# Per-head query norms of an attention layer: two root-mean squares taken in one PSUM bank and spread by copies, rotation ahead of the plain part

## What is computed

```python
def rms_norm(x, gain):
    y = xf * lax.rsqrt(jnp.mean(xf * xf, axis=-1, keepdims=True) + RMS_EPS)
    return (y * gain).astype(x.dtype)

q = (rms_norm(c_q, q_norm_g) @ w_qb).reshape(B, S, H, 192)
q = rms_norm(q, q_head_g)                    # per head, over all 192 features
q = concatenate([q[..., :128], rope(q[..., 128:], pos)], axis=-1)
# k likewise (one rotated part for all heads); logits = q k^T / sqrt(192),
# block-causal mask, softmax over k, times v
```

## Time and profile before

| | us |
|---|---|
| median of 3 runs | 4075.6 |
| lowest and highest run | 4072.52, 4077.5 |
| the profiled execution | 4080.59 |
| span of its slowest core (core 2) | 4079.6 |
| spans of the other cores | 4057.6 to 4076.4 |
| granted TensorE clock, mean of core 2 | 0.988 of full |

### The profile page before, as it was taken

The page is one execution under the profiler, slowest core; times in us unless marked ns, Lnnn a source line. Parts: engine busy times, 40 slices in busy tenths (PEclk is TensorE's granted clock), DMA queues, the critical chain, the costliest instruction groups (busy, mean ns, idle before and its releaser), DMA issues.

```text
span 4079.6 us, 62233 instructions; the slowest of 8 cores (4057.6 to 4079.6 us)
## 1 busy us (share of the span) xinstructions
PE 3846.2 (94%) x20843; PEld 1921.3 (47%) x21232; DVE 2096.5 (51%) x3814; ACT 1610.6 (39%) x2538; POOL 664.8 (16%) x746
## 2 busy tenths in 40 slices
PE   6999999999988889999999999999999898889999
PEld 3455554444435454444454554544444454544444
DVE  4444437737354446727534445475473544467272
ACT  2433334313257574403233332542232666644130
POOL 1233221010011011110023234110000111200000
PEclk8999999999999999999999999999999999999999
DMA  6222123454321111665451231243533201214643
GB/s 152 43 56 56 27 41 50 73 91 70 66 59 32 22 35 24 97 134 109 99 126 27 49 67 24 43 68 64 91 61 68 51 27 27 53 32 77 130 72 84
DMA packets 92469, 262.77 MB, mean 64 GB/s; under 512 B 8704, under 2 KB 9856, under 8 KB 92160
## 3 DMA queue, kind: packets, MB, share of 16 engines
q0 software_dynamic: 57824, 184.84, 27.4%
q1 hardware_dynamic: 34336, 73.93, 5.7%
HBM read 426.77 MB, written 16.78 MB: 109 GB/s over the span
## 4 chain that ended last, share of the span: by engine, by line
PE 86%; ACT 4%; issue 4%; DVE 3%; DMA 2%; POOL 1%; SPq 0%; ACTq 0%; DVEq 0%; POOLq 0%
PE psum L365 83%; PE psum L1119 2%; ACT m_P L368 2%; DMA ring<-wts 1%; DVE hT L374 1%; POOL r_u L378 1%; DMA xT<-xin 1%; ACT m_sqq L368 1%; ACT m_rsq L368 1%; ACT n_sq L368 0%; DVE m_ot L371 0%; DVE m_kn L381 0%; SPq L243 0%; DVE xT L371 0%; DVE r_P L374 0%
## 5 line engine op out<-in xcount | busy, mean ns | idle before, releaser
L365 PE MATMUL psum<-hT,ring 128*128 128x512 bf16 x7915 | 1784.6, 382 | 47.2 <-DMA ring<-wts 17.9
L365 PEld LDWEIGHTS psum<-hT,ring 128*128 128x128 bf16 x8064 | 788.9, 98 | 1007.2 <-issue 77.8
L371 DVE TENSOR_TENSOR xT<-xT,psum 128x512 f32<-128x512 f32 x512 | 350.3, 686 | 688.9 <-PE psum L365 667.4
L368 ACT ACTIVATE f_c<-psum,prm_s 128x512 f32<-128x512 f32 x352 | 273.3, 777 | 1036.0 <-PE psum L365 1025.2
L374 DVE SCALAR_TENSOR_TENSOR f_c<-psum,prm_s,f_c 128x511 f32<-128x511 f32 x704 | 526.8, 748 | 258.2 <-ACT f_c L368 209.1
L365 PE MATMUL psum<-f_uT,ring 128*128 128x512 bf16 x2766 | 607.5, 379 | 2.6
L243 POOL DMA_DIRECT2D ring<-wts x390 | 208.4, 541 | 2059.1 <-PE psum L365 1955.7
L368 ACT ACTIVATE m_P<-psum,m_rstdk 128x512 bf16<-128x512 f32 (+3 forms) x640 | 386.0, 626 | 137.7 <-PE psum L1119 128.4
L365 PEld LDWEIGHTS psum<-f_uT,ring 128*128 128x128 bf16 x2816 | 274.9, 98 | 332.8
L365 PE MATMUL psum<-r_u,ring 128*128 128x512 bf16 x976 | 242.9, 379 | 6.8 <-DVE xT L371 2.6
L1119 PE MATMUL psum<-m_v,m_P 128*128 128x129 bf16 x2176 | 234.9, 221 | 13.9 <-DVE m_ot L371 12.3
(11 more groups left out here) (111 smaller groups left out, 3103.4 us busy)
## 6 DMA issues: line engine op xcount, KB each, us to landing
ring<-wts POOLq DMA_DIRECT2D x250, 512.0 KB, 7.4
ring<-wts POOLq DMA_DIRECT2D x128, 352.0 KB, 4.5
m_rope<-mrope SPq DMA_DIRECT2D x40, 512.0 KB, 4.2
xT<-xin SPq DMA_DIRECT2D x32, 512.0 KB, 15.6
r_rt<-rrope SPq DMA_DIRECT2D x32, 512.0 KB, 3.8
xout<-xT SPq DMA_DIRECT2D x32, 512.0 KB, 7.2
ring<-wts POOLq DMA_DIRECT2D x4, 1024.0 KB, 11.5
ring<-wts POOLq DMA_DIRECT2D x8, 288.0 KB, 4.2
```

The lines of the kernel that those rows point to most:

```text
L365: return kb.op('pe', lambda e: e.matmul(out, lhsT, rhs, start=start, stop=stop), reads, writes, signal)
L368: return kb.op('act', lambda e: e.activation(out=out, in_=in_, func=func, **kw), reads, writes)
L371: return kb.op('dve', lambda e: e.tensor_tensor(out=out, in0=a, in1=b, op=op), reads, writes)
```

## The change

`sums` becomes one stage: `halves[:, a]` has ones in 64 of its columns, so the plain squares of head 0 are summed to partitions 0 to 63 and those of head 1 to partitions 64 to 127 of the same bank; `blocks`, two blocks of ones on the diagonal, adds the rotated parts. One Ln and one Exp give both heads' factors in `rstd`, a tile that other parts of the kernel use at other times. Four DMA copies of 64 partitions x 2 KB on SP's queue, emitted behind the Exp, write head a's factors to both halves of `rsq[:, a]`. `scale_r` is one operation of 128 partitions that reads `rstd` and needs no copy. `turn` and an empty stage follow, and only then the two plain scalings, as two stages. A chain has 12 stages: project, two squares, sums, root, empty, scale_r, turn, empty, scale_n(0), scale_n(1), rope. `halves` and `blocks` are made by memsets instead of being loaded, so the table `misc` is loaded without its last 256 columns, and the key's rotated sums read `blocks`.

```diff
-        halfa = sb("halfa", [128, 128], BF16)
-        halfb = sb("halfb", [128, 128], BF16)
+        halves = sb("halves", [128, 2, 128], BF16)
+        blocks = sb("blocks", [128, 128], BF16)
...
+        kb.op('dve', lambda e: e.memset(halves[:], 0.0), writes=[onesb])
+        kb.op('dve', lambda e: e.memset(blocks[:], 0.0), writes=[onesb])
+        for a in range(2):
+            r = slice(64 * a, 64 * a + 64)
+            kb.op('dve', lambda e, a=a, r=r: e.memset(halves[:, a, r], 1.0), writes=[onesb])
+            kb.op('dve', lambda e, r=r: e.memset(blocks[r, r], 1.0), writes=[onesb])
...
-                    MM(pr[:, b:b + 1], sqkr[:, b * 128:(b + 1) * 128], halfa[:, 0:1], True, True, [sqkrb, constb], [prb],
+                    MM(pr[:, b:b + 1], sqkr[:, b * 128:(b + 1) * 128], blocks[:, 0:1], True, True, [sqkrb, onesb], [prb],
...
-            rsqb = [ar.buf('m_rsq%d' % a, 36 + 2 * a, 2) for a in range(2)]
+            rsqa = [ar.buf('m_rsq%d' % a, 36 + 2 * a, 2) for a in range(2)]
+            rsqh = [[Buf('m_rsqh%d%d' % (a, r)) for r in range(2)] for a in range(2)]
...
-                def sums(a):
+                def sums():
                     bi = rots(); held.insert(0, bi)
                     ps, psb = bank(bi)
-                    MM(ps, ones[:], sqq[:, a, :], True, False, [sqqb[a], onesb], [psb], signal=False)
-                    MM(ps, (halfa, halfb)[a][:], sqq[:, 2, :], False, True, [sqrb, constb], [psb])
+                    for a in range(2):
+                        MM(ps, halves[:, a, :], sqq[:, a, :], a == 0, False, [sqqb[a], onesb], [psb], signal=False)
+                    MM(ps, blocks[:], sqq[:, 2, :], False, True, [sqrb, onesb], [psb])
 
                     def log():
                         held.remove(bi)
-                        ACT(rsq[:, a, :], ps, AF.Ln, [psb], [rsqb[a]], bias=EPS, scale=1.0 / 192)
+                        ACT(rstd[:], ps, AF.Ln, [psb], [rstdb], bias=EPS, scale=1.0 / 192)
                     later.append(log)
 
-                def root(a):
-                    later.append(lambda: ACT(rsq[:, a, :], rsq[:, a, :], AF.Exp, [rsqb[a]], [rsqb[a]], scale=-0.5))
+                def root():
+                    def fn():
+                        ACT(rstd[:], rstd[:], AF.Exp, [rstdb], [rstdb], scale=-0.5)
+                        for a in range(2):
+                            for r in range(2):
+                                kb.dma('sp', 'rs%d%d' % (a, r), rsq[64 * r:64 * r + 64, a, :], rstd[64 * a:64 * a + 64, :],
+                                       reads=[rstdb], writes=[rsqh[a][r]])
+                    later.append(fn)
 
                 def scale_r():
-                    for a in range(2):
-                        r = slice(a * 64, a * 64 + 64)
-                        STT(xg0[r, :], psum[r, 7, :], prm[r, P_QHR:P_QHR + 1], rsq[r, a, :], ALU.mult, ALU.mult,
-                            [pb[7], prmb, rsqb[a]], [xgb[0]])
-
-                def scale_n():
-                    for a in range(2):
-                        STT(Qn[:, s, a, :], psum[:, 5 + a, :], gqk[:], rsq[:, a, :], ALU.mult, ALU.mult,
-                            [pb[5 + a], gqkb, rsqb[a]], [qnb[s][a]])
+                    STT(xg0[:], psum[:, 7, :], prm[:, P_QHR:P_QHR + 1], rstd[:], ALU.mult, ALU.mult,
+                        [pb[7], prmb, rstdb], [xgb[0]])
+
+                def scale_n(a):
+                    STT(Qn[:, s, a, :], psum[:, 5 + a, :], gqk[:], rsq[:, a, :], ALU.mult, ALU.mult,
+                        [pb[5 + a], gqkb] + rsqh[a], [qnb[s][a]])
...
-                stages.extend([project, lambda: square(0), lambda: square(1), lambda: sums(0), lambda: sums(1), lambda: root(0), lambda: root(1),
-                               none, scale_r, scale_n, turn, none, rope])
+                stages.extend([project, lambda: square(0), lambda: square(1), sums, root, none, scale_r, turn, none,
+                               lambda: scale_n(0), lambda: scale_n(1), rope])
...
-        miscf = ar.tensor("miscf", [128, 768], F32, 100); miscb = ar.buf('misc', 100, 3)
-        kb.dma('sp', 'misc', miscf[:], misc_d, writes=[miscb])
+        miscf = ar.tensor("miscf", [128, 512], F32, 100); miscb = ar.buf('misc', 100, 2)
+        kb.dma('sp', 'misc', miscf[:], misc_d[:, 0:512], writes=[miscb])
...
-        for dst, c0 in ((identb, 256), (negmb, 384), (rotb, 128), (halfa, 512), (halfb, 640)):
+        for dst, c0 in ((identb, 256), (negmb, 384), (rotb, 128)):
```

More of the change, by code:

```diff
@@ L907, in mla_layer @@
             sqqb = [ar.buf('m_sqq%d' % a, 96.5 + a, 1) for a in range(2)]; sqrb = ar.buf('m_sqr', 98.5, 1)
[L908 removed]
+            rsqa = [ar.buf('m_rsq%d' % a, 36 + 2 * a, 2) for a in range(2)]
+            rsqh = [[Buf('m_rsqh%d%d' % (a, r)) for r in range(2)] for a in range(2)]
+            for a in range(2):
+                for r in range(2):
+                    kb.handoff(rsqh[a][r], [rsqa[a]])
             otb = [ar.buf('m_ot%d' % i, 102.5 + i, 1) for i in range(2)]
@@ L970, in rope @@
                 def rope():
-                    PTT(rsq[:, 0, :], xg0[:], mrope[:, 0, :], ALU.mult, [xgb[0], mropeb], [rsqb[0]])
-                    TT(rsq[:, 1, :], psum[:, 7, :], mrope[:, 1, :], ALU.mult, [pb[7], mropeb], [rsqb[1]])
-                    PTT(Qr[:, s, :], rsq[:, 0, :], rsq[:, 1, :], ALU.add, rsqb, [qrb[s]])
+                    PTT(rsq[:, 0, :], xg0[:], mrope[:, 0, :], ALU.mult, [xgb[0], mropeb], rsqh[0])
+                    TT(rsq[:, 1, :], psum[:, 7, :], mrope[:, 1, :], ALU.mult, [pb[7], mropeb], rsqh[1])
+                    PTT(Qr[:, s, :], rsq[:, 0, :], rsq[:, 1, :], ALU.add, rsqh[0] + rsqh[1], [qrb[s]])
                     made[0] = n + 1
                     if n == 15:
+                        for a in range(2):
+                            for r in range(2):
+                                kb.handoff(rsqa[a], [rsqh[a][r]])
                         ring_i[0] += 7
```

## The result

| | before | after |
|---|---|---|
| median on the same chips, us | 4077.9 | 4068.8 |
| ratio, 95% interval | 1 | 0.9972 [0.9961, 0.9983] |
| profiled execution, us | 4080.59 | 4066.09 |
| PE busy, slowest core, us | 3846.2 | 3831.4 |
| first attention stage, us | 163.9 | 163.7 |

Some runs of both kernels fell into a slower state, in which half of the cores or all of them are granted a lower clock; the medians count these runs, while the ratio compares the others alone and is the figure to go by, not the 9.1 us between the medians. By the ratio the change makes the kernel 0.28% faster, 11.5 us in 4078, between 7 and 16. The forecast was 24.5 us. The sign was right and the time lies in the range, but the size is half, and the place is another one: 23.0 of the 24.5 were to come from attention, which gave nearly nothing.

What follows compares the result with a forecast made beforehand. PE, busy 94% of 4079.6 us, was taken as the bound. Attention 23.0, key and value stages 3.2, copies -1.2, layer's end -1.0 and start 0.5 sum to 24.5 us, taking the median 4075.6 to 4051; range 4038 to 4075.

Steps and rivals of the forecast that it cites:

- 23.0 us for attention: In the attention stages, 28 chains would each save 0.82 us from the removed Ln and Exp: 23.0 us.
- ACT, 0.82 us a chain: In attention, losing one Ln and one Exp turns steps of 1.05 and 1.09 us into 0.66 each, saving 0.82 us.
- PE, "inside the 0.82", counted at nothing: In attention, the removed sums matmul, 0.22 us, lies in ACT's stretch and adds nothing to the 0.82 us a chain.
- The merged sums and the order, counted at "shortens nothing": Chains having 12 stages instead of 13 would by itself shorten nothing, since the number of steps is fixed.
- The copies, 1.2 us: Copies land just in time for scale_n; 0.1 us charged at each of 12 chains following without a gap: -1.2 us.
- The rivals with slow copies: Late copies delay scale_n: at half rate 4073 us, chance 0.10; at 8.4 us a copy 4120 us, chance 0.09.
- The forecast's 243 GB/s with room to spare: Copies of 128 KB issued every 0.54 us on SP need 243 GB/s, which the DMA engines would keep up with.
- Key and value stages, 3.2 us in four: One DVE multiplication fewer in the key and value stages saves 0.8 us in each of four: 3.2 us.
- Start, 0.5: At the kernel's start, a table 128 KB shorter in front of x saves 0.5 us, at most 1.4.
- Stages near the layer's end, -1: Near the layer's end, m_on behind scalings costs, earlier output chunks gain: together -1 us, between -4 and +3.
- the one named in that step at 0.7: Near the layer's end, one cast of m_on behind two next-norm scalings delays an S bank some 0.7 us, four times.
- The rival "ACT's time was slack": In attention, shorter ACT steps only move PE's waits, so only the matmul counts: 7 us, 4068.6 us, chance 0.12.

Runs made afterwards that it cites:

- one root: Kernel before with each chain's second Ln and Exp left out, head 1 scaled with head 0's factors: ratio 0.9971, first attention stage 160.7 us.
- one sum: Kernel before without each chain's second Ln and Exp, and also without the second group of sums (two matmuls): ratio 0.9933, first attention stage 157.05 us.
- old order, no copies: Changed kernel without its four copies, scale_n reading rstd, in the stage order of the kernel before: ratio 0.9905, first attention stage 158.7 us.
- no copies: Changed kernel without its four copies, both plain scalings reading rstd directly: ratio 0.9941, first attention stage 161.5 us.
- the early waits: Changed kernel with ACT waiting for the last chain's copies before the chain's first square instead of at Ln: ratio 0.9961, first attention stage 162.0 us.
- the first experiments: Runs beginning with the kernel before without each chain's second Ln and Exp (0.9971), then also without the second group of sums (0.9933).
- the experiment with the scalings apart: Changed kernel with empty stage before sums, ACT's copy waits early, turn later, and next norm's scalings moved clear of POOL's squares: 0.9927, median 4051.9 us.

## Why the prediction was wrong

The first attention stage adds up from the runs, in us:

| part | us | from | second sequence, us |
|---|---|---|---|
| second Ln and Exp gone | -3.2 | one root: 160.7 - 163.9 | -2.9 |
| second group's two matmuls gone | -3.6 | one sum: 157.05 - 160.7 | -3.9 |
| third matmul, and its wait for the second square | +1.6 | old order, no copies: 158.7 - 157.05 | +2.0 |
| the new order of stages | +2.8 | no copies: 161.5 - 158.7 | +2.5 |
| the copies | +2.1 | changed: 163.6 - 161.5 | +3.1 |
| sum | -0.3 | | +0.8 |

The last column is the same stage of the second sequence in the same runs (163.9, 161.0, 157.1, 159.1, 161.6 and 164.7 us): the same parts with the same signs, and the copies dearer. So the forecast's largest term, 23.0 us for attention, failed in two steps. It took ACT's saving for 0.82 us a chain where it is 0.46, and it put the merged sums and the new order at nothing where they take 4.4 us a stage.

*ACT, 0.82 us a chain: the step that failed first.* It read two step lengths of the earlier trace rows and set them back to 0.66. It left out what follows in the same rows: the four m_P behind the chain take 2.50 us, which less the last one's 0.69 is 3 x 0.60. These steps run faster than PE's pace of 0.66, so the stretch before had let work queue up, and part of each long step was repaid behind it, 0.18 us in these three. Removing the Ln and Exp removes the repayment too, and leaves ACT waiting for PE, as the one-root timeline shows. Measured: 0.46.

*PE, "inside the 0.82", counted at nothing.* 0.52 us a chain for two matmuls. Here PE and ACT take turns at being last, so neither's work covers the other's: with ACT's part gone, PE's gave its full time on top. By itself this error helped; 0.46 + 0.26 for one matmul would have been 0.72, near the forecast 0.82, but for a reason that was not given.

*The merged sums and the order, counted at "shortens nothing".* This is the largest miss, 2.8 us a stage for the order and most of 1.6 for the sums. I counted stages and did not lay the new ones on the timeline. It could have been done with rows I had. A square stands behind its step's exponential and ends 0.15 us after the next exponential has begun (1208.32 + 0.62 against 1208.79 in the earlier trace rows; timeline of ACT before)

```profile
1208.32 0.62 ACT L368 ACTIVATE m_sqq<-psum 128x512 bf16<-128x512 f32 x1
```

while PE is free for the next stage's matmuls once it has the bank that the last exponential left; sums(0) needed the square of the step before, the merged sums need this last one. And sums and root in adjoining ticks put Ln and Exp behind adjoining exponentials. An empty stage on either side of the sums brought back 1.9 and 2.6 us.

*The copies, 1.2 us.* The landing was right, 2.3 against 2.4. The cover was thinner than forecast: DVE's m_qn waited for a copy in each of the stage's 7 chains, 6.1 us together and 2.2 at the longest, where the scalings were to come just in time. But PE never waited for m_qn there, and with the early waits, which leave 6.4 us of DVE's waits, the copies cost 0.5 us a stage. Most of what they cost went where I had not looked, to the other end of the copies' life: four more semaphores ahead of the next Ln, of which I had asked only "who waits for the copies' data", not "who waits before overwriting what they read". The rivals with slow copies fell with the landing time.

What the copies moved is seen in a window of the changed kernel, to be held against the earlier trace rows:

```profile
1209.00:1211.00 2.00, 2.00 (x19) 1.27 (x18) 0.47 (x1) 1.81 (x4) 0.00 (x0) 1.00 0.91 208
```

The DMA engines were busy for 0.91 of it at 208 GB/s, where the load over 128 partitions moved 252 at 0.89. The forecast's 243 GB/s with room to spare was too high. SP alone, with 0.6 us from one issue to the next, would hold copies of 128 KB to about 220 GB/s, so the window can't tell whether SP or the half of the partitions set the rate. The Trainium skill (SBUF — State Buffer, "Can I just issue two DMAs to hit both halves?") has two such transfers run one after the other; at the 196 GB/s that the prediction takes from the Trainium skill one copy needs 0.67 us, an estimate, and copies that are issued 0.6 us apart neither bear this out nor refute it.

*Key and value stages, 3.2 us in four.* From the first cast of m_kn to the first exponential the four are 1.2, 1.5, 1.3 and 1.3 us shorter, 5.3 in all. Between the first sequence's halves only 0.3 us of it are left, because the stretch from the last exponential to the first cast of m_kn took 6.4 to 6.7 us instead of 5.45 where the granted clock fell to its lower level in it, on three cores before and on six after. The place was right and the size wasn't: 1.3 a stage is more than the 0.8 that DVE's multiplication can give, and no run says what gives the rest.

*Start, 0.5.* 0.2 measured at the first layer's first matmul, on the slowest cores.

*Stages near the layer's end, -1.* PE's wait of 3.5 us on xT went, and a wait on m_on of 3.9 us took its place, the one named in that step at 0.7. Its real size is that m_on stood behind a scaling stretched by POOL. Net about nothing.

*The rival "ACT's time was slack"* gave 4068.6, which is the measured 4068.8, but not by its mechanism: ACT's time was not slack, it was worth 3.2 us a stage and was given back elsewhere. That the whole time lies in the stated range is luck as well: losses that the forecast did not have took back nearly all that attention gained.

Placed are thus some 6.6 us: 5.3 in the key and value stages, 1.1 in the four attention stages (0.3, 0.3, -0.8 and 1.3, the second and the last with drops of the clock in them) and 0.2 at the start. The other 5 of the 11.5 lie in stages with the same instructions before and after, which differ between profiles by as much; whether they belong to the change stays open. In the two profiled executions the mean granted clock, median of the cores, is 0.9905 before and 0.992 after, an estimated 6 us; over the runs that the ratios compare there is no such difference (0.9906 after, and 0.9906 for the kernel before on the chip of the first experiments), so the clock explains the profiles and not the ratio.

## What to carry to other kernels

When two engines take turns at being last, lay every moved or merged stage on the timeline step by step, up to where the pace is normal again: steps faster than the normal pace behind a stretch are its repayment and must be taken off the saving. For a DMA that reads a shared tile, cost the next writer's waits as well as the reader's, and put them where that engine has time; that alone returned 1.5 to 1.7 us a stage. Before two runs are compared by the length of a stage, see on each core whether the granted clock was full in it: here a drop at its start was worth as much as the effects under test. Before merging two stages, see whether the merged one now needs the later of two producers.

## What the runs showed of the hardware

Waits on semaphores that are long satisfied are not free: four of them ahead of ACT's Ln took 0.22 us, 55 ns each, visible only as the distance from the last matmul's start to the Ln, 0.69 against 0.47 in one chain, and 0.75 against 0.53 with and without the copies as the median of all chains.

A stretch of lower granted clock at the start of an attention stage (0.50 of full in 1201.00 to 1202.80 on core 3 before) made the stage 1.7 us longer, 165.6 against 163.9.

DVE's scaling of hT, 0.74 us, took 2.78 and 4.08 us while POOL squared the next tile of xT in operations of 3.6 us, of which the second took 4.05; the eight together took 10.76 us, and 5.4 us clear of POOL. DVE's additions to xT, whose second operand is in PSUM, stayed at 0.69 us beside the same squares (at 1540.85 and 1542.38 us in the experiment with the scalings apart, POOL at work from 1537.30 to 1544.46). The Trainium skill (SBUF — State Buffer, "SBUF: two separate sides") says that DVE and GpSimd share a pair of ports which one instruction holds for its whole length, and that a DVE operation with two SBUF inputs takes part against a GpSimd operation that reads SBUF. By that rule, the trace agrees: xT and nrs are two such inputs, and 4.08 less 0.74 is 3.3 us, nearly a whole operation of POOL.
